# Strassen weight sums moved from POOL to DVE, with a reordered opening of the last pair, an earlier load of the mixed inputs and an earlier third convolution

## What is computed

```python
u = rms_norm(h, g_mix);  q, k, v, a, b = split(u @ w_in)
glu = a * sigmoid(b)
att = band_attend(q, k, v)                       # 8 heads, chunks of 64
cv  = silu(layer_norm(causal_depthwise_conv31(glu) + conv_b))
h = h + concatenate([att, cv]) @ w_out
u = rms_norm(h, g_ffn)
gate, up = split(u @ w_gate_up)                  # D_FF = 2816
h = h + (silu(gate) * up) @ w_down
g = sigmoid(rms_norm(h, g_ple) @ w_ple_gate)
h = h + g * (p @ w_ple_proj)
```

## Time and profile before

| | before |
|---|---|
| runs | 2650.25, 2646.38, 2649.82 us; median 2649.82 us |
| profiled execution | 2649.25 us, span 2647.5 us |
| mean granted clock | 0.997 |
| TensorE busy | 2621.2 us, 99% |
| DVE, ACT, POOL busy | 1719.8, 1191.7, 292.3 us |

### The profile page before, as it was taken

One profiled execution on the slowest core, in us unless ns is written; L12 is line 12 of the kernel. 1 busy time (PEld: TensorE's weight loads), 2 busy tenths in 40 slices (PEclk: granted clock), 3 DMA queues, 4 the chain that ended last, 5 costly groups with the idle time before them and its releaser, 6 DMA issues.

```text
span 2647.5 us, 40104 instructions
## 1 busy us (share of the span) xinstructions
PE 2621.2 (99%) x14504; PEld 2565.8 (97%) x14504; DVE 1719.8 (65%) x3159; ACT 1191.7 (45%) x2192; POOL 292.3 (11%) x277
## 2 busy tenths in 40 slices
PE   9999999999999999999999999999998999999999
PEld 8999999999999999999999999999998999999999
DVE  4555478988978888776747885876547344343452
ACT  5444367877763323443234344233445243243453
POOL 6222200000001111111111111110002000000000
PEclk9999999999999999999999999999999999999999
DMA  5667798788578988898888878897784454454677
GB/s 200 211 217 233 255 348 272 267 275 278 187 242 262 299 290 291 284 322 293 311 283 294 293 268 280 311 310 267 257 286 136 143 169 136 139 172 134 189 240 237
DMA packets 336593, 654.07 MB, mean 247 GB/s; under 512 B 35564, under 2 KB 204396, under 8 KB 335852
## 3 DMA queue, kind: packets, MB, share of 16 engines
q1 hardware_dynamic: 336396, 651.50, 73.9%
HBM read 501.70 MB, written 151.71 MB: 247 GB/s over the span
## 4 chain that ended last, share of the span: by engine, by line
PE 88%; DVE 6%; DMA 3%; ACT 2%; issue 1%; POOL 1%; SPq 0%; POOLq 0%; DVEq 0%; ACTq 0%
PE psum L198 53%; PE psum L2199 25%; PE psum L1509 3%; PE psum L1485 2%; DVE y L2771 2%; PE psum L1473 1%; PE psum L1472 1%; DMA x<-in_w_out 1%; DVE wres L2725 1%; ACT wres L2603 0%; POOL wres L628 0%; DMA a_cr<-in_cache 0%; DMA rstd<-in_w_in 0%; PE psum L837 0%; DVE ul L685 0%
## 5 line engine op out<-in xcount | busy, mean ns | idle before, releaser
L198 PE MATMUL psum<-uh,wres 128*128 128x416 f32 x3936 | 1118.9, 356 | 7.9 <-DVE ul L2788 3.8
L198 PEld LDWEIGHTS psum<-uh,wres 128*128 128x128 f32 x3936 | 737.7, 188 | 20.2 <-DVE ul L2788 4.6
L198 PE MATMUL psum<-ul,wres 128*128 128x416 f32 x1968 | 688.3, 350 | 0.0
L2603 ACT ACTIVATE wres<-x 128x1024 fp32r<-128x1024 f32 (+2 forms) x234 | 268.5, 1148 | 644.8 <-PE psum L198 593.9
L198 PE MATMUL psum<-wres 128*128 128x416 f32 x2304 | 447.6, 352 | 1.8 <-ACT wres L2603 1.5
L198 PEld LDWEIGHTS psum<-wres 128*128 128x128 f32 x2304 | 430.4, 188 | 8.9 <-issue 1.9
L2199 PE MATMUL psum<-wres 128*128 128x416 f32 x1992 | 396.5, 353 | 7.4 <-ACT wres L1631 7.4
L2199 PEld LDWEIGHTS psum<-wres 128*128 128x128 f32 x1992 | 375.1, 189 | 11.8 <-ACT wres L1631 7.8
L198 PEld LDWEIGHTS psum<-ul,wres 128*128 128x128 f32 x1968 | 370.8, 188 | 6.8 <-issue 1.6
L2771 DVE SCALAR_TENSOR_TENSOR y<-c_top,vec,y 128x416 f32<-128x416 f32 (+1 forms) x600 | 319.8, 601 | 0.7
L1631 ACT ACTIVATE wres<-c_top 128x512 fp32r<-128x512 f32 (+1 forms) x282 | 168.6, 599 | 174.4 <-PE psum L2199 127.6
(11 more groups left out here) (254 smaller groups left out, 3136.8 us busy)
## 6 DMA issues: line engine op xcount, KB each, us to landing
x<-in_w_gu SPq DMA_DIRECT2D x132, 512.0 KB, 4.8
wres<-w_gu_lo SPq DMA_DIRECT2D x88, 512.0 KB, 5.6
c_top<-in_w_gu SPq DMA_DIRECT2D x154, 256.0 KB, 5.1
x<-in_w_down SPq DMA_DIRECT2D x48, 704.0 KB, 5.8
w_gu_lo<-wres SPq DMA_DIRECT2D x44, 512.0 KB, 6.2
w_gu_sums<-c_top SPq DMA_DIRECT2D x44, 512.0 KB, 6.0
wres<-w_down_lo SPq DMA_DIRECT2D x32, 704.0 KB, 7.0
c_top<-w_gu_sums SPq DMA_DIRECT2D x88, 256.0 KB, 2.9
```

The source lines that it names most:

```text
L198: mm = nc.tensor.matmul(out, w[wp](kw), u[up](ku), start=first and n == 0 and j == 0, stop=last and n == len(kts) - 1 and j == 2)
L2603: nc.scalar.activation(whi[v % 2][:, 0:kts, :], raw[v % 2][:, 0:kts, :], ACT.Copy).then_inc(hi_done, 1)
```

## The change

Five things change. DVE makes the four weight sums of a piece in place of POOL, at unit v + 1 for a piece loaded at step v, ahead of that unit's taps. SP's loads and stores of these pieces follow a table, `sums_of`: piece n is loaded at step 8 + 196 n // 44 and stored three steps later. In the pair, the opening order moves P6 2 and P7 0 ahead of P5 0; t1 and t4 are made by DVE, later; the low and high parts of t3 are made ahead of those of t1 and b22; P7's eviction for tile 0 moves behind P3 1. The third convolution runs 13, 13 and 2 rounds in the units D, P and the first two of Y/O, where it ran 11, 11 and 6 (over all Y/O units). The high halves of the mixed inputs go to another place in SBUF (`wide`), loaded at P 3 and P 5 of block 2; the low halves stay at the Y unit.

```diff
-OPENING = ("P1 0", "P2 0", "P1 1", "P2 1", "P1 2", "P2 2", "P1 3", "P2 3", "P6 0", "P6 1", "P5 0", "P5 1", "P3 0", "P3 1",
-           "P7 0", "P6 2", "P4 0", "P5 2", "P7 1", "P6 3", "P4 1", "P3 2", "P5 3", "P7 2", "P3 3", "P4 2")
+OPENING = ("P1 0", "P2 0", "P1 1", "P2 1", "P1 2", "P2 2", "P1 3", "P2 3", "P6 0", "P6 1", "P6 2", "P7 0", "P5 0", "P5 1",
+           "P3 0", "P3 1", "P4 0", "P5 2", "P7 1", "P6 3", "P4 1", "P3 2", "P5 3", "P7 2", "P3 3", "P4 2")
...
-def weight_sums(nc, c):
+def weight_sums(nc, dve, c, n):
...
-    @c["block"].gpsimd
-    def _(pool):
-        for n in range(2 * KF):
-            pool.wait_ge(came, SUM_IN + 32 * (n + 1))
-            nc.gpsimd.tensor_tensor(a22, a21, a22, ALU.add).then_inc(made, 1)
...
+    dve.wait_ge(came, SUM_IN + 32 * (n + 1))
+    nc.vector.tensor_tensor(a22, a21, a22, ALU.add).then_inc(made, 1)
+    dve.wait_ge(made, SUM_MADE + 4 * n + 1)
+    nc.vector.tensor_tensor(a21, a21, a11, ALU.subtract).then_inc(made, 1)
+    dve.wait_ge(made, SUM_MADE + 4 * n + 2)
+    nc.vector.tensor_tensor(a11, a22, a11, ALU.subtract).then_inc(made, 1)
+    dve.wait_ge(made, SUM_MADE + 4 * n + 3)
+    nc.vector.tensor_tensor(a12, a12, a11, ALU.subtract).then_inc(made, 1)
...
             if i == 6:
                 for k in K4:
-                    u_low("t1", k, t1l[k], t1r[k], t1h[k])
+                    less(t1r[k], b12r[k], uar[k], ("ub", k))
             if i == 7:
                 for k in K4:
-                    u_low("b22", k, b22l[k], b22r[k], b22h[k])
...
+                    dve.wait_ge(made, MT + k + 1)
+                    dve.wait_ge(u_raw, raw_at["t3", k])
+                    nc.vector.tensor_tensor(t4r[k], dr[k], t3r[k], ALU.add).then_inc(u_raw, 1)
...
         for n, u in enumerate(us):
             op, j, m, i = u["op"], u.get("j"), u.get("m"), n - start
-            low(n + 2)
             if n:
                 after(n - 1)
+            low(n + 2)
...
-            3: spread(2, places("U", 1, 1, (10,))) + spread(11, places("D", 1, 1)) + spread(11, places("P", 1)) + spread(
-                6, out_units),
+            3: spread(2, places("U", 1, 1, (10,))) + spread(13, places("D", 1, 1)) + spread(13, places("P", 1)) + spread(
+                2, out_units[0:2]),
...
+        SUMS_FROM, SUMS_TO = 8, 208
+        sums_of = {SUMS_FROM + (SUMS_TO - SUMS_FROM - 4) * n // (2 * KF): n for n in range(2 * KF)}
...
-                    first, last = (4 * KF * (v + e - SUMS_FROM) // (SUMS_TO - SUMS_FROM) for e in (0, 1))
-                    for n in range(first, last):
-                        if n % 2:
-                            sums_store(sp, c, s, n // 2)
-                        else:
-                            sums_load(sp, t, c, n // 2)
+                    if v - 3 in sums_of:
+                        sums_store(sp, c, s, sums_of[v - 3])
+                    if v in sums_of:
+                        sums_load(sp, t, c, sums_of[v])
...
+                if kind == "P" and b == SINGLE - 1 and u["m"] in (3, 5):
+                    half = KH * (u["m"] == 5)
+                    first = 9 * KH * P + half * N
                     sp.wait_ge(c["mix_out"][0], MIX0 + 32)
...
+                    sp.wait_ge(used, U0 + unit_at("D", b, KD - 1, 1) + 1)
+                    second_mix(wide[:, first:first + KH * N].rearrange("p (k n) -> p k n", n=N), s["mh"], half)
...
+                if v - 1 in sums_of:
+                    weight_sums(nc, dve, c, sums_of[v - 1])
                 if v in first_taps:
                     first_tap(first_taps[v])
                 for n, r in taps_of[v]:
                     taps(n, r)
```

More of the change, by code:

```diff
@@ L1703, in last_pair @@
     sa_of = {n: j for j, n in sa_at.items()}
+    ub_at = {j: at["P7", j] if j else at["P3", 1] for j in range(KF)}
+    ub_of = {n: j for j, n in ub_at.items()}
     left_order, sig_order, hid_order, kept_order = [], [], [], []
@@ L1931, in _ @@
                 high("t2", i - 3, "t2", t2h[i - 3], t2r[i - 3])
[L1932 to L1933 removed]
             if i == 7:
                 for k in K4:
[L1936 removed]
+                    act.wait_ge(u_raw, raw_at["t1", k])
+                    copy(t3h[k], t3r[k], u_hi)
             if i == 8:
                 for k in K4:
[L1939 removed]
+                    high("t1", k, "t1", t1h[k], t1r[k])
             if i == 9:
                 for k in K4:
[L1942 removed]
+                    high("b22", k, "ub4", b22h[k], b22r[k])
+            if i == 10:
+                for k in K4:
+                    high("t4", k, "t4", t4h[k], t4r[k])
             if op == "O" and u["h"]:
@@ L2075, in p_low, with low @@
                                     ALU.subtract).then_inc(p_lo, 1)
+        def low(n):
+            if n >= NP or not us[n]["summed"]:
+                return
+            dve.wait_ge(hi_done, H + n + 1)
+            dve.wait_ge(used, U + n - 3)
+            nc.vector.tensor_tensor(f["lo"][slot(n)], f["raw"][(n + 2) % 3], raw(f["hi"][n % 4]), ALU.subtract).then_inc(lo_done, 1)
         def second_sums(i):
@@ L2209, in _ @@
         PB = [(pbh[k], pbl[k]) for k in range(KD)]
-        MIX = [(hx[:, k, :], hx[:, KD + k, :]) for k in range(KD)]
+        MIX = [(tile(k), hx[:, KD + k, :]) for k in range(KD)]
         for n, u in enumerate(us):
@@ L2531, in gw_load, with second_mix @@
                     sp.dma_start(gw[:, :, HIST + cut:], rows[:, :, HIST + SEQ:]).then_inc(gw_in, 16)
-            SUMS_FROM, SUMS_TO = 8, 208
+            wide = c["wres"][:, :, :].rearrange("p s e -> p (s e)")
+            def second_mix(dst, src, half):
+                sp.dma_start(dst.bitcast(F32), src.rearrange("(k p) n -> p k n", p=P)[:, half:half + KH, SECOND * N:(SECOND + 1) * N]
+                             ).then_inc(mix_in, 16)
             GW_AT = {("D", 0, 1, 3): 2, ("G", 1, 1, 2): 3, ("G", 2, 0, 2): 4}
@@ L3022, in _ @@
                     cv_total(early(u), int(u["f"] == 4))
-        weight_sums(nc, c)
         last_pair(nc, t, c, s, f)
```

99 lines of the change are left out of this document (39 added, 60 removed).

## The result

The changed kernel takes 2696.88 us, the median of 4 runs from 2693.21 to 2702.62; the kernel before takes 2650.03 in the same comparison. The ratio is 1.0176, with an interval of 1.0164 to 1.0189: 46.9 us slower. The forecast was 2677, with a range to 2695.

A forecast was written before the change was run, and what follows sets the result against it. TensorE, busy 2621.2 of 2647.5 us, was taken as the bound. From 2649.25, adding 27, 7 and 2.5 and subtracting 6.7 and 1.5 gave 2677.6, stated as 2677 us; 8-in-10 range 2652 to 2695.

The forecast's parts named there:

- Block 0's wait for the piece, +27: Block 0: DVE stands for the piece's load, so its low weights reach TensorE late; 27 us lost in all.
- 4 x 3.9: Block 0's four U units with sums: TensorE gets low weights 3.9 us late in each, before store terms.
- Its clock, +7: Block 0: a lower clock after each of the four long stalls, 1.7 us each, 7 us lost.
- rival 3: Stalls starve the next weight load and the clock drops longer: 35 + 12 in block 0, +8 at the convolution; 2697 us, chance 0.13.
- Blocks 1 and 2: 0: Blocks 1 and 2: no loss, as DVE makes no low weights there and banks come free three units ahead.
- The third convolution, +2.5: Third convolution: late pieces delay DVE and TensorE, less a clock gain; 2.5 us lost, bounds -5.5 and +8.
- the second wait: Third convolution, O units: TensorE loses 2 us there, besides some 1 us at each of P 5 to P 7.
- the half clock: Third convolution: the slow clock after the long wait for the low part would go, winning 1.7 us.
- The opening, -6.7: The pair's opening: the first wait and its slow clock go, 10.3 us, less 3.6 at later products; 6.7 us won.
- Mixed inputs, -1.5: The pair's first O units: loading half the inputs earlier removes TensorE's wait, winning 1.5 us.
- The credit for collisions, 1.95 us a piece: Taps slow by about 1.95 us when meeting POOL's sums, so DVE's 1.7 us of sums is nearly free.
- the signs named ahead: Expected in the profile: 9 to 11 low-weight waits in block 0, longest about 5 us; DVE's DMA waits; opening waits under 1 us.

The follow-up runs named there:

- e2: The changed kernel with DVE's sums one unit later, at v + 2 instead of v + 1: 2647.08 us, ratio 0.9987 to the kernel before.
- e3: The changed kernel with the sums back on POOL, while DVE still waits for the piece's DMAs at v + 1 without summing: 2692.08 us, ratio 1.0154.
- e4: The changed kernel with DVE's sums at v + 1 only for pieces loaded below step 68, POOL making the others: 2685.37 us, ratio 1.0124.
- e5: The kernel of e2 with the third convolution's rounds as before the change (11, 11 and 6): 2645.80 us, ratio 0.9985.
- e7: The kernel before with only the sums moved to DVE at v + 1 and the changed table of loads and stores: 2702.40 us, ratio 1.0200.
- e8: The kernel before with only the pair's opening and the mixed inputs changed, sums on POOL: 2644.43 us, ratio 0.9982.
- e9: The kernel of e2 with another table, pieces loaded every four steps from 12 to 132 and from 154 to 202: 2637.85 us, ratio 0.9948.
- e10: The kernel of e9, same table, with the sums on POOL instead of DVE: 2635.88 us, ratio 0.9948.

## Why the prediction was wrong in size

**Block 0's wait for the piece, +27: right, by partly other numbers.** DVE's low weights were waited for 28.1 us in 11 waits (2.0 before), and 0.8 us was lost at `c_hl_last` after them: +26.9 (28.1 with the gaps too short to be listed). The sum is partly luck, since the parts differ. The U units at 834, 857, 1034 and 1057 us lost 6.3, 3.1, 3.5 and 2.8 us, 15.6 as in 4 x 3.9; the G units 6.7 for 8.0 with their store terms; the D units 3.6 for 1.8; and 2.1 us came at v = 9, where I had nothing and where there was no DMA wait, only work. e2 and e3 show the cause named, the wait and not the work.

**Its clock, +7: too small.** The same matmuls took 9.9 us longer. I counted four drops at 1.7 us, one in each U unit. There were five, at 2.0 us each in the mean: in three of the U units (834, 857 and 1034 us) and in two G units (902 and 1006 us), where I had counted none; the 2.81 us wait of the fourth U unit and the 3.59 us one of a D unit had none. This is rival 3's half about the clock, at part of its 12 us. That rival's total, 2697, is the measured time, but by luck: it had 47 in block 0, where 38 were lost, and nothing for the stretches between block 0 and the third convolution, where 6.4 were.

**"Blocks 1 and 2: 0": this step failed.** Measured are +6.0 and +0.4. It argued that low weights no longer come from DVE there, put DVE's wait at 2 us or so (it was 5.3 us at 1187), and looked only at TensorE's direct needs. By e4 the 6 us go with DVE's sums outside block 0. The path is ACT's queue (8.83 us for DVE's eviction, the next weights behind it).

**The third convolution, +2.5: bounds right, size and reason off.** +6.9, within the bound of 8. My waits of 1 us at P 5 to P 7 are there (2.6 us in three), as is the second wait (1.69 and 3.52 us), but I had the half clock go, and it stayed; and I took the new spread for a gain. By e5 it is none, by e4 and e7 the loss is that of the sums.

**The opening, -6.7: too large.** -4.4, or -3.4 by e8. The 3.6 us for the products behind P6 0, until P3 1, were right: 0.93, 0.92, three times 0.43 and 0.41 make 3.55. Two terms were put at nothing. P6 0 itself still waits for 1.25 us (2008.9 against 2008.4 in my sum would be 0.5, and it was not charged), and P7's moved eviction costs 1.75. With them 6.55 us are idle, and 10.3 less that is 3.75, against 4.4 and 3.4 measured. The Trainium skill, SBUF — State Buffer, section SBUF: two separate sides, has DVE and GpSimd block each other fully at their shared ports; four low parts of 128x416 took 2.09 us here without POOL, and one alone 1.48 beside it, so the trace agrees that DVE wins by POOL's absence. Part of what it won in speed it spent on eight more instructions, two groups of 2.09 us.

**Mixed inputs, -1.5: right.** -1.8 to -2.3 in all runs that have it, -0.5 in e7, which has not.

**The credit for collisions, 1.95 us a piece: true where they meet, seldom otherwise.** The prediction's 4.28 us and 2.33 us are both in the trace. But all 600 tap instructions together took 319.8 us before and 293.2 after, 26.6 us less or 0.6 us for each of 44 pieces. The Trainium skill, Perfetto Trace Analysis, section Optimizing Scalar/DVE Operations, says that moving work between GPSIMD and DVE may not help since they share a read port; e9 and e10, at 0.9948 both, agree.

Of the signs named ahead, the 11 waits for low weights and DVE's waits in front of L1673 (36 of them, 3.1 us on average) came; the longest was 6.3 us, not 5, and the opening has idle times of over 1 us.

In sum, over the forecast: 4.0 in block 0 (38.0 less 27 + 7), 6.4 from there to the third convolution, 4.4 in it, 2.3 in the opening, less 0.6 at the mixed inputs and 0.9 in parts that the change leaves alone. That is 15.6 us, and the profiled execution took 2693.21 us where the sum said 2677.6; the median lies 3.7 above it.

## What to carry to other kernels

Before work moves from an idle engine to a busy one, ask what it waits for, not how long it takes: the same 176 instructions cost 50 us directly behind a DMA and nothing one unit later. Where an in-order engine stands, follow each of its consumers, and what is queued behind them in their own queues, until TensorE is reached. A wait of TensorE for a low part can be a shortage of DVE over the 100 us before it; move other work out of that stretch, since a new spread of the same work only moves the wait.

## What the runs showed of the hardware

- A wait alone cost nearly as much as wait and work (1.0154 and 1.0176). With POOL at work the landing of a DMA started POOL and DVE together: four taps that stood right behind the wait took 4.32 us, not 2.33.
- Store and load of one place in SBUF, one step apart, chain to 5.91 + 6.50 us of DMA and 6.2 us of DVE: 19.4 us from the issue of the store at 814.70 to TensorE at 834.05, a little more than four units of 4.5 us.
- Waits of TensorE of 2.91 and 6.29 us were followed by stretches at a mean granted clock of 0.54 and 0.74 over 7 us, and in e2 one of 2.07 us by 0.76 over 7 us. Waits of 2.81 and 3.59 us were not (1.00). So the length of a wait alone did not tell. In e10, whose longest wait after 780 us is 1.3 us, the clock over the whole span is 1.000.
